# Activations and gates of a block in one piece of memory, and sixteen blocks gated ahead

## The reference

```python
def peer_ffn(h, w_query, sub_keys, expert_u, expert_v):
    ...
        q = (hc @ w_query).reshape(chunk, PEER_HEADS, PEER_QDIM)
        s1 = jnp.einsum('thd,nd->thn', q[..., :half], k1)
        s2 = jnp.einsum('thd,nd->thn', q[..., half:], k2)
        v1, i1 = lax.top_k(s1, PEER_TOPK)
        v2, i2 = lax.top_k(s2, PEER_TOPK)
        cand = ...                       # v1 + v2 of all 16 x 16 pairs
        sc, pos = lax.top_k(cand, PEER_TOPK)
        eidx = jnp.take_along_axis(cidx, pos, axis=-1)
        g = jax.nn.softmax(sc, axis=-1)
        u = jnp.take(expert_u, eidx, axis=0)
        a = jnp.einsum('thkd,td->thk', u, hc)
        act = jax.nn.gelu(a, approximate=False) * g
        vv = jnp.take(expert_v, eidx, axis=0)
        return jnp.einsum('thk,thkd->td', act, vv)
```

## Time and profile before

| | |
|---|---|
| median of 3 runs | 2956.66 us |
| profiled execution | 2956.8 us |
| its span | 2955.0 us |
| granted clock of TensorE | 0.998 |
| PE busy | 2925.4 us, 99% |
| DVE busy | 1557.3 us, 53% |
| ACT busy | 1131.7 us, 38% |
| POOL busy | 1564.9 us, 53% |
| HBM | 405.97 MB read, 61.05 MB written |

### The profile page before, as it was taken

The page is one execution under the profiler, slowest core; times in us unless marked ns, Lnnn a source line. Parts: engine busy times, 40 slices in busy tenths (PEclk is TensorE's granted clock), DMA queues, the critical chain, the costliest instruction groups (busy, mean ns, idle before and its releaser), DMA issues.

```text
span 2955.0 us, 38907 instructions
## 1 busy us (share of the span) xinstructions
PE 2925.4 (99%) x14774; PEld 2514.6 (85%) x14774; DVE 1557.3 (53%) x2599; ACT 1131.7 (38%) x1646; POOL 1564.9 (53%) x1002
## 2 busy tenths in 40 slices
PE   9999999999999999999999999999999999999998
PEld 7887888888888888899999997778888888888887
DVE  5826347889982222478888864363111436631213
ACT  6556344433332323333333334454223344432332
POOL 6731443888887770277777304634444433444442
PEclk9999999999999999999999999999999999999999
DMA  4244942445445455799999943222333321123332
GB/s 149 95 141 146 313 158 85 133 141 148 145 145 147 143 151 184 262 343 376 368 369 363 356 131 114 72 72 95 98 100 93 112 72 65 51 93 100 94 99 86
DMA packets 269428, 473.32 MB, mean 160 GB/s; under 512 B 39460, under 2 KB 173508, under 8 KB 268760
## 3 DMA queue, kind: packets, MB, share of 16 engines
q1 hardware_dynamic: 234456, 403.79, 41.5%
q0 software_dynamic: 34816, 67.41, 6.5%
HBM read 405.97 MB, written 61.05 MB: 158 GB/s over the span
## 4 chain that ended last, share of the span: by engine, by line
PE 95%; issue 1%; DVE 1%; POOL 1%; DMA 1%; ACT 0%; SPq 0%; DVEq 0%; POOLq 0%; ACTq 0%
PE pb L899 30%; PE pb L900 30%; PE pb L901 30%; PE pb L1499 1%; PE pb L1080 1%; POOL s_over L748 0%; PE pb L1179 0%; PE pb L1108 0%; PE pb L1340 0%; DMA s_ring<-w 0%; PE pb L1360 0%; PE pb L1047 0%; PE pb L1261 0%; PE pb L1349 0%; PE pb L947 0%
## 5 line engine op out<-in xcount | busy, mean ns | idle before, releaser
L748 POOL TENSOR_TENSOR s_over<-s_ring,s_rhigh 128x1024 fp32r<-128x1024 f32 x271 | 660.0, 2438 | 952.8 <-ACT s_rhigh L1607 952.3
L1607 ACT ACTIVATE s_rhigh<-s_ring 128x1024 fp32r<-128x1024 f32 x525 | 556.1, 1060 | 1224.1 <-DMA s_ring<-w 498.3
L899 PE MATMUL pb<-s_over,s_rhigh 128*128 128x512 f32 (+1 forms) x2392 | 877.5, 367 | 0.8 <-DVE s_over L2293 0.6
L900 PE MATMUL pb<-s_over,s_rhigh 128*128 128x512 f32 (+1 forms) x2392 | 873.8, 365 | 0.0
L901 PE MATMUL pb<-s_over,s_over 128*128 128x512 f32 (+1 forms) x2392 | 873.8, 365 | 0.0
L899 PE MATMUL pb<-s_hS,s_rhigh 128*128 128x512 f32 (+1 forms) x1664 | 650.0, 391 | 5.3 <-DVE s_hS L2785 2.5
L901 PE MATMUL pb<-s_hS,s_over 128*128 128x512 f32 (+1 forms) x1672 | 645.3, 386 | 0.0
L900 PE MATMUL pb<-s_hS,s_rhigh 128*128 128x512 f32 (+1 forms) x1664 | 642.2, 386 | 0.0
L809 POOL DMA_INDIRECT gates<-s_arena x384 | 467.8, 1218 | 116.9 <-issue 116.9
L2293 DVE TENSOR_TENSOR s_over<-s_ring,s_rhigh 128x1024 fp32r<-128x1024 f32 x254 | 310.6, 1223 | 383.3 <-ACT s_rhigh L1607 382.9
L899 PEld LDWEIGHTS pb<-s_over,s_rhigh 128*128 128x128 f32 x2392 | 449.4, 188 | 55.0 <-DVE s_over L2293 1.0
(11 more groups left out here) (302 smaller groups left out, 2818.9 us busy)
## 6 DMA issues: line engine op xcount, KB each, us to landing
s_ring<-w SPq DMA_DIRECT2D x272, 512.0 KB, 3.3
s_ring<-eu SPq DMA_DIRECT2D x128, 512.0 KB, 3.9
s_ring<-ev SPq DMA_DIRECT2D x128, 512.0 KB, 5.8
acts<-s_arena SPq DMA_DIRECT2D x128, 256.0 KB, 3.9
gates<-s_zero SPq DMA_DIRECT2D x24, 1024.0 KB, 7.5
s_arena<-acts SPq DMA_DIRECT2D x128, 192.0 KB, 5.1
s_arena<-gates SPq DMA_DIRECT2D x128, 192.0 KB, 6.3
gates<-s_arena POOLq DMA_INDIRECT x384
```

What stands on the lines that cost most here:

```text
L748: gp.tensor_tensor(rlow[:, s, :, :], ring[:, s, :, :], rhigh[:, s, :, :].bitcast(F32), ALU.subtract).then_inc(S("w_split"), 1)
L899: mm(dst, a_high, b_high, start=start, stop=False)
L900: mm(dst, a_high, b_low, start=False, stop=False)
L1607: sc.activation(rhigh[:, s, :, :], ring[:, s, :, :], ACT.Copy).then_inc(S("w_high"), 1)
```

## The change

The two arrays in memory, activations and gates, become one, `pairs`, in which each block and row has 384 activations and behind them its 384 gates (3072 B). Four things follow.

1. `act_in` reads both in one transfer of 384 KB into one buffer, `pin`.
2. `act_out` writes two transfers, the activations of the 384 dense tokens into `pairs` and those of the 128 sparse tokens into an array of their own, `few`, which takes over the memory of the old table. The indices that DVE computes change to match (factors 2·TD and NS in place of TD and T).
3. The zeroing covers every second stretch of 1536 B. It is done in 32 transfers of 768 KB, two behind each of 16 weight tiles.
4. `PREP` = 16 blocks are gated during the last 16 tiles of the up half. SP waits for all scatters behind the load of tile 112 and then fetches one block behind each `eu` load; ACT rounds one gated block behind each GELU; DVE does one gating and one low part beside each weight. The first eight loads of `ev` after the seam then come without a fetch of activations.

```diff
+NS = P
+ZW, ZQ = TD // 2, 16
+PREP = 16
-ZW, ZN, ZQ = 256, 8, 24
...
-        acts = nc.dram_tensor("acts", (NK, P, T), F32, kind="Internal").ap()
-        acts1 = acts.rearrange("n p (t one) -> (n p t) one", one=1)
+        pairs = nc.dram_tensor("pairs", (NK, P, 2, TD), F32, kind="Internal").ap()
+        gate1 = pairs.rearrange("n p two (t one) -> (n p two t) one", one=1)
+        few = gates.rearrange("b n p t -> (b n p t)")[0:NK * P * NS].rearrange("(n p t) -> n p t", p=P, t=NS)
...
-                sp.dma_start(gzero[q], zero[:, :].unsqueeze(1).to_broadcast([P, NK * NK * TD // (ZQ * P * ZW), ZW]))\
-                    .then_inc(S("table_zero"), 16)
+                for h in range(2):
+                    sp.dma_start(pairs[8 * q:8 * q + 8, :, 1, h * ZW:(h + 1) * ZW].rearrange("n p c -> p n c"),
+                                 zero[:, :].unsqueeze(1).to_broadcast([P, 8, ZW])).then_inc(S("table_zero"), 16)
...
-                sp.dma_start(va_in[:, k % 4, 0:TD], acts[bass.ds(n, 1), :, 0:TD].rearrange("n p t -> p (n t)"))\
-                    .then_inc(S(f"a_in{k % 4}"), 16)
-                sp.dma_start(gtile[:, k % 4, 0:TD], gtab[bass.ds(n, 1)].rearrange("n p t -> p (n t)"))\
-                    .then_inc(S(f"a_in{k % 4}"), 16)
+                sp.dma_start(pin[:, k % 4, :, :].rearrange("p two t -> p (two t)"),
+                             pairs[bass.ds(n, 1)].rearrange("n p two t -> p (n two t)")).then_inc(S(f"a_in{k % 4}"), 16)
...
-                sp.dma_start(acts[k], ua[:, k % 4, :]).then_inc(S(f"a_out{k % 4}"), 16)
+                sp.dma_start(pairs[k, :, 0, :], ua[:, k % 4, 0:TD]).then_inc(S(f"a_out{k % 4}"), 16)
+                sp.dma_start(few[k], ua[:, k % 4, TD:T]).then_inc(S(f"a_out{k % 4}"), 16)
...
-            for t in range(TT - 1):
-                sp.wait_ge(S(f"g_put{t}"), 16 * PH * TOPK)
-            for e in range(4):
-                sp.wait_ge(S(f"a_out{e}"), 32)
-                act_in(e, e)
+                if k == NK - PREP:
+                    for t in range(TT - 1):
+                        sp.wait_ge(S(f"g_put{t}"), 16 * PH * TOPK)
+                    for e in range(4):
+                        sp.wait_ge(S(f"a_out{e}"), 32 * PREP // 4)
+                if k >= NK - PREP:
+                    e = k - (NK - PREP)
+                    if e >= 4:
+                        sp.wait_ge(S("e_raw"), e - 3)
+                    act_in(e, e)
...
-                sp.wait_ge(S("e_raw"), r + 1)
-                act_in(4 + r, 4 + r)
-            for e in range(4):
-                sp.wait_ge(S(f"a_out{e}"), 16 * 32)
-            for r in range(4):
-                sp.wait_ge(S("e_raw"), r + 5)
-                act_in(r, 8 + r)
-            with sp.Fori(0, 7) as g:
-                for r in range(16):
+                sp.wait_ge(S("e_raw"), PREP + r - 3)
+                act_in(r, PREP + r)
+
+            for r in range(PREP - 8):
+                tile(T_V + r + 4, a["ev"][r + 4])
+            with sp.Fori(0, 6) as g:
+                for r in range(PREP - 8, PREP + 8):
...
-                if k >= 125:
-                    for e in ((0, 1), (2, 3), (4, 5, 6, 7))[k - 125]:
-                        gated_high(e)
+                if k >= NK - PREP:
+                    gated_high(k - (NK - PREP))
...
-            while lowered[0] < T_V:
+            while lowered[0] <= T_V - PREP + 1:
                 low_next()
-            for k in range(8):
+            for k in range(PREP):
                 gated(k)
                 if k >= 1:
                     gated_low(k - 1)
-                if k % 2:
-                    low_next()
-            gated_low(7)
-            gated(8)
+                low_next()
+            gated_low(PREP - 1)
+            while lowered[0] < T_V + RING:
+                low_next()
```

More of the change, by code:

```diff
@@ L407, in program @@
         shares = nc.dram_tensor("shares", (8, T), F32, kind="Internal").ap()
-        acts = nc.dram_tensor("acts", (NK, P, T), F32, kind="Internal").ap()
-        acts1 = acts.rearrange("n p (t one) -> (n p t) one", one=1)
+        pairs = nc.dram_tensor("pairs", (NK, P, 2, TD), F32, kind="Internal").ap()
+        gate1 = pairs.rearrange("n p two (t one) -> (n p two t) one", one=1)
+        few = gates.rearrange("b n p t -> (b n p t)")[0:NK * P * NS].rearrange("(n p t) -> n p t", p=P, t=NS)
+        few1 = few.rearrange("n p (t one) -> (n p t) one", one=1)
         rows = a["ev"].rearrange("n e c o -> (n e) (c o)")
[L411 to L414, removed]
         actS = Area().take(2, 2, 8, T, dt=F32R)
@@ L453, in program @@
         at_same = C.at
-        va_in = C.take(4, TD)
-        gtile = C.take(4, TD)
+        pin = C.take(4, 2, TD)
         vrow = [Area(NA * 2 * TD + 1024 * i).take(1024) for i in range(4)] + [C.take(1024) for i in range(2)] +\
@@ L694, in _ @@
                     act_in(r, g * 16 + (r + 12))
+            for r in range(104, 112):
+                tile(T_V + r + 4, a["ev"][r + 4])
+                sp.wait_ge(S("e_raw"), r + 9)
+                act_in(r, r + 12)
             sp.dma_start(pT, a["pT"]).then_inc(S("masks_in"), 16)
@@ L798, in _ @@
             splits(T_QUERY, U_LOW)
-            gp.wait_ge(S("table_zero"), 16 * ZQ)
+            gp.wait_ge(S("table_zero"), 32 * ZQ)
             for h in range(PH):
@@ L824, in pick_act @@
                     gp.wait_ge(S("sp_mul"), j // 16 - 1)
-                gp.indirect_dma_start(s_act[:, j:j + 1], None, acts1,
+                gp.indirect_dma_start(s_act[:, j:j + 1], None, few1,
                                       bass.IndirectOffsetOnAxis(ap=s_el[:, j:j + 1], axis=0))\
@@ L832, in _ @@
             for e in range(4):
-                gp.wait_ge(S(f"a_out{e}"), 16 * 32)
+                gp.wait_ge(S(f"a_out{e}"), 32 * 32)
             for i in range(4):
@@ L1779, in gelu @@
                 if k >= 4:
-                    sc.wait_ge(S(f"a_out{k % 4}"), 16 * (k // 4))
+                    sc.wait_ge(S(f"a_out{k % 4}"), 32 * (k // 4))
                 sc.activation(ua[:, k % 4, :], pb[:, k % 4, :], ACT.Gelu).then_inc(S("e_read"), 1)
@@ L1798, in _ @@
                     gate_exp(EXP_AT.index(k))
-                if k >= 125:
-                    for e in ((0, 1), (2, 3), (4, 5, 6, 7))[k - 125]:
-                        gated_high(e)
+                if k >= NK - PREP:
+                    gated_high(k - (NK - PREP))
             for r in range(8):
                 parts(T_V + r + 3)
-                gated_high(8 + r)
             with sc.Fori(0, 6) as g:
@@ L2354, in _ @@
             for t in range(TT):
-                m = ve.tensor_tensor_reduce(sbk[:, t, :], mat(M_ID), iota, 1.0, float(t * P), ALU.mult,
+                m = ve.tensor_tensor_reduce(sbk[:, t, :], mat(M_ID), iota, 1.0, float(TD + t * P if t < TT - 1 else 0), ALU.mult,
                                             ALU.add, tok[:, t:t + 1])
@@ L2451, in _ @@
                 ve.wait_ge(S("at_step"), 3 * i + 1)
-                ve.scalar_tensor_tensor(g_atf, chosen[:, 0:TT - 1, picks], float(TD),
+                ve.scalar_tensor_tensor(g_atf, chosen[:, 0:TT - 1, picks], float(2 * TD),
                                         tok[:, 0:TT - 1].unsqueeze(2).to_broadcast([P, TT - 1, 16]),
@@ L2465, in _ @@
             ve.tensor_copy(s_row, chosen[:, TT - 1, :]).then_inc(S("s_listed"), 1)
-            ve.scalar_tensor_tensor(flat, chosen[:, TT - 1, :], float(T), tok[:, TT - 1:TT].to_broadcast([P, P]),
+            ve.scalar_tensor_tensor(flat, chosen[:, TT - 1, :], float(NS), tok[:, TT - 1:TT].to_broadcast([P, P]),
                                     ALU.mult, ALU.add).then_inc(S("s_listed"), 1)
@@ L2485, in gated @@
             def gated(e, g=0):
-                ve.wait_ge(S(f"a_in{e % 4}"), g * 128 + 32 * (e // 4 + 1))
+                ve.wait_ge(S(f"a_in{e % 4}"), g * 64 + 16 * (e // 4 + 1))
                 if e >= 2:
                     ve.wait_ge(S("e_act"), g * 16 + (e - 1))
-                ve.tensor_tensor(std[:, e % 2, 0:TD], va_in[:, e % 4, 0:TD], gtile[:, e % 4, 0:TD], ALU.mult)\
+                ve.tensor_tensor(std[:, e % 2, 0:TD], pin[:, e % 4, 0, :], pin[:, e % 4, 1, :], ALU.mult)\
                     .then_inc(S("e_raw"), 1)
@@ L2522, in _ @@
                     gated_low(k - 1)
-                if k % 2:
-                    low_next()
-            gated_low(7)
-            gated(8)
+                low_next()
+            gated_low(PREP - 1)
+            while lowered[0] < T_V + RING:
+                low_next()
             assert lowered[0] == T_V + RING
             for r in range(NK):
-                if r + 9 < NK:
+                if PREP <= r + 9 < NK:
                     gated(9 + r)
@@ L2532, in _ @@
                     weight_low(T_V + r + 3)
-                if r + 8 < NK:
+                if PREP <= r + 8 < NK:
                     gated_low(8 + r)
```

## The result

| | before | after |
|---|---|---|
| median | 2956.79 us (21 runs) | 2962.53 us (21 runs) |
| lowest to highest | 2955.16 to 2959.86 | 2960.69 to 2965.33 |
| ratio | | 1.0020, 95% interval 1.0014 to 1.0026 |
| profiled execution | 2956.8 us | 2964.6 us |

The change makes the kernel 5.7 us slower. That is just on the bound of 0.2%: a small loss, clear of zero, in the place that the prediction named and larger than its 2.8 us.

What follows compares the result with a forecast made beforehand. PE was taken to bound the kernel. From 2956.8 us profiled, -0.6 at the seam and +3.4 for zeroing gave 2959.6, or 2959.5 us as median: no measurable change, on the slow side; range 2955.5 to 2972 us.

Steps and rivals of the forecast that it cites:

- no gain over 0.64 us can come: Whole kernel: PE has only one wait, 0.64 us, where the change acts, so no more can be given back.
- The up half and the down half cost nothing: Up half: the added DVE and SP work fits; down half: same bytes in one transfer per block; neither costs time.
- Rival 3: Down half: a 384 KB transfer holds up the `ev` load behind it; 9 us lost, 2965 us; chance 0.05.
- -0.6 us at the seam, because sixteen blocks are ready: Start of the down half: eight loads follow without fetches between them, so the 0.64 us PE wait goes.
- The zeroing makes a tile dearer than PE's 4.99 us: Gate stage: a tile with its zeroing needs 5.62 us of the DMA queue; PE waits 3.4 us.
- 15C - 80.9: Gate stage: PE's wait in us by tile 16, C being each tile's DMA queue need; waits start at C = 5.39.
- Rival 1: Gate stage: a deep queue keeps C at or under 5.39, so PE never waits; 2956.1 us; chance 0.21.
- C = 5.62 us: Gate stage: DMA queue need per tile, 1.45 us load plus 4.17 us zeros, giving a 3.4 us PE wait.
- Rival 2: Gate stage: short, scattered packets or extra transfers starve PE, from C = 5.83; 2968.2 us at C = 6.2; chance 0.34.
- the 4.4 that would have made it wrong: Gate stage: the forecast counts as wrong if zeroings of 768 B take over 4.4 us per pair.
- its bound of 5.9 us: Whole kernel: 0.2%, the least difference a measurement can tell from no change; reached at a wait of 6.5 us.

Runs made afterwards that it cites:

- the run with the spread zeroing: The changed kernel with one 768 KB zeroing transfer behind each of 32 weight tiles, not two behind each of 16: 2955.55 us, ratio 0.9998.
- the run with 1 KB packets: The kernel before with its zeroing behind 16 tiles, 1.5 MB each, in contiguous 1 KB packets: 2961.27 us, ratio 1.0014.

## Why the prediction was right, and where it was off

- *PE bounds the kernel, and no gain over 0.64 us can come.* Right in kind, a little short in size. The gain was 0.94 us. The row of a wait leaves a part of it out: in the five profiles that have this wait, the stretch is longer than 1226.75 us by the wait and 0.3 us more (0.5 in one).
- *The up half and the down half cost nothing.* Right: no PE wait from 400 to 1500 us, and the run with the spread zeroing has the time of before. Rival 3 is refuted.
- *-0.6 us at the seam, because sixteen blocks are ready.* The number is near (0.94 us), its reason right in part. That the late load was the cause is shown; but sixteen ahead isn't needed for it, and the prediction missed SP's wait for the last activations, which was in its diff.
- *The zeroing makes a tile dearer than PE's 4.99 us, and the prefetch is used up before tile 16.* Right, and 15C - 80.9 gives the wait from C in five runs. Rival 1 is refuted.
- *C = 5.62 us.* This is the step that was off; it measured 5.81, and 0.19 us fifteen times is 2.9 of the 3.0 us that were missing. It has two parts. First, the level, 0.12 us: the load and the megabyte of zeros were read as 1.45 + 2.75 us from two passes between landings; measured with 1 KB packets over 15 tiles, the sum is 5.70 and not 5.58. Second, the packet, 0.08 us: a line through packets of 1 and 4 KB put 1.5 ns on each packet apart from its bytes, 0.04 us per tile, and the step from 1 KB to 768 B measured 0.12. The line's far point was not sharp enough for the nanosecond that hangs on it: of the 17343 packets in the earlier trace rows only 12693 can be rows of 4 KB, and the time of the others is in the 178 ns; if they took 20 ns each (an assumption), the line would give 4.0 ns in place of 1.5. On the other side, the weight loads from 450 to 500 us before take some 190 ns per row (23.1% of 800 us for 964 rows of 4 KB and 124 short packets), by which nothing would be left apart from the bytes. Whether the level was off by the chance of two passes or because a deeper queue is slower is not separated: in the run with 1 KB packets, stretches of 4.2 us between 280 and 360 us run at 347 to 389 GB/s, so that two passes at 374 lie inside of the spread. The Trainium skill ("DMA: Bandwidth & Descriptors", Why small descriptors are slow) would have the zeros of 768 B 2.9% dearer than those of 1 KB; the rows here give 3.1% (4.38 against 4.25 us, with 1.45 us for the load taken off both). For 512 B it gives 8.6% and the rows 18.6%. Its line-rate from 512 B up (Specifications) does not hold for these writes.
- *Rival 2, short and scattered packets.* Its first half is a part of what happened (0.12 us of C), its second is refuted: 128 KB apart costs 0.01 us.
- *The chances.* 0.39 for a loss beyond 0.2%, with 2956 to 2962 as the likeliest range; the measured 2962.53 lies half a microsecond outside of the latter, on the side of rival 2. By the prediction's own signs it is a draw: the interval between landings, 5.81 us, is just over the 5.8 that it gave to rival 2, and the pair of zeroings, 4.36 us (5.81 less 1.45), is just under the 4.4 that would have made it wrong. That the loss of 5.7 us came out under its bound of 5.9 us for a measurable one, and not over it, is luck: the interval reaches to both sides.

## What to carry to other kernels

Work that is hidden behind a stage has a density as well as a size. The same 25 MB cost nothing at 1 MB per tile and 6.5 us at 1.5 MB, so before moving hidden transfers work out the need of the queue per step against the step's own time, and how many steps the prefetch can lend. Take the rate for that from a stretch where the queue is full for long: here two passes between landings gave 374 GB/s, and 15 tiles 368. And keep such packets at 1 KB or more.

When a change brings the gain that was expected of it, take its parts away one by one all the same: here two lines of the old code, a wait wider than its reads needed, held all of it.

## What the runs showed of the hardware

- SP's own issue slows when the queue is deep. A load's issue took 0.33 us before and takes 3.0 to 3.8 us once zeroing has queued up, as in these rows of the changed kernel:

```profile
276.48 1.05 SPq L532 DMA_DIRECT2D s_ring<-w  x1
...
309.30 3.82 SPq L532 DMA_DIRECT2D s_ring<-w  x1
```

- The DMA engines' rate in a full queue is 368 GB/s with 1 KB writes between the loads, 360 with 768 B and 323 with 512 B (2.097 MB by C), and their share of the time reads 1.06 to 1.08 in all three. A share over 1 says that the queue is full, not what it moves.
- With PE's waits of 3 to 5 us, about 11 us apart, the granted clock falls to windows of 0.60 to 0.72, and the last such wait costs more than its length, by up to 2.8 us. Waits of up to 1.97 us, 6 to 18 us apart, left it at 1.00. In between, waits of 2.93 and 2.15 us were followed by a lower clock and one of 2.34 us was not.
